# HGRN2 stage: the diagonals of the heads' own scores on ScalarE, behind the squares of the head in front, in place of VectorE

## What is computed

```python
q, fz, i, g = jnp.split(x @ w_in, 4, axis=-1)
q = jax.nn.silu(q)
f = lower_bound + (1.0 - lower_bound) * jax.nn.sigmoid(fz)
log_f = jnp.log(f)
k = 1.0 - f
...
rel = b[:, :, :, None, :] - b[:, :, None, :, :]
decay = jnp.exp(jnp.where(causal[:, :, None], rel, -jnp.inf))
scores = jnp.einsum('bhtk,bhsk,bhtsk->bhts', qc, kc, decay)
intra = jnp.einsum('bhts,bhsv->bhtv', scores, vc)
...
o = rms_norm(o, g_norm).reshape(B, S, D_MODEL) * jax.nn.silu(g)
return o @ w_o
```

## Time and profile before

| | |
|---|---|
| median of 3 runs | 968.34 us (968.09 to 968.36) |
| the profiled execution, its time | 967.88 us |
| its span | 966.1 us |
| granted TensorE clock, mean over the span | 0.999 of full speed |
| TensorE busy | 956.1 us, 99% |
| VectorE busy | 848.8 us, 88% |
| ScalarE busy | 564.8 us, 58% |
| GpSimd busy | 37.9 us, 4% |

### The profile page before, as it was taken

How to read it: one execution, slowest core, us unless ns; L and a number is a source line. 1 busy time by engine, 2 the same in 40 slices (tenths; PEclk the granted TensorE clock), 3 DMA queues, 4 the chain that set the end, 5 groups by cost and what they waited for, 6 DMA issues and landing times.

```text
span 966.1 us, 12770 instructions
## 1 busy us (share of the span) xinstructions
PE 956.1 (99%) x4520; PEld 792.9 (82%) x4520; DVE 848.8 (88%) x1208; ACT 564.8 (58%) x627; POOL 37.9 (4%) x64
## 2 busy tenths in 40 slices
PE   9999999999999999999999999999999999999996
PEld 7888888888888888888888888888888888888885
DVE  5999888996888999899899998999898998888896
ACT  6665556436645555565565555549898545565650
POOL 0100000000210000000000000000100100000000
PEclk9999999999999999999999999999999999999999
DMA  9686566553657565665566565735233655565631
GB/s 305 221 267 239 195 199 222 190 181 125 225 196 237 179 213 179 213 217 174 177 216 216 174 218 179 257 113 192 88 132 121 228 196 193 180 215 176 214 133 43
DMA packets 129312, 184.47 MB, mean 191 GB/s; under 512 B 5968, under 2 KB 104800, under 8 KB 129136
## 3 DMA queue, kind: packets, MB, share of 16 engines
q1 hardware_dynamic: 126032, 173.56, 54.5%
q0 software_dynamic: 2672, 9.77, 2.8%
q10 hardware_dynamic: 560, 0.52, 0.2%
HBM read 182.78 MB, written 1.05 MB: 190 GB/s over the span
## 4 chain that ended last, share of the span: by engine, by line
PE 95%; DVE 3%; ACT 1%; issue 0%; DMA 0%; POOL 0%; DVEq 0%; ACTq 0%
PE psum L1711 29%; PE psum L1720 29%; PE psum L1715 29%; PE psum L1886 2%; PE psum L2235 1%; PE psum L1704 1%; PE psum L2221 1%; DVE w_lo L937 0%; DMA raw<-in_ffn_w_in 0%; ACT w_hi L482 0%; PE psum L1970 0%; PE psum L1990 0%; PE psum L2207 0%; DVE w_lo L967 0%; PE psum L2039 0%
## 5 line engine op out<-in xcount | busy, mean ns | idle before, releaser
L937 DVE TENSOR_TENSOR w_lo<-raw,w_hi 128x2048 fp32r<-128x2048 f32 x125 | 284.8, 2282 | 7.5 <-ACT w_hi L482 7.3
L1711 PE MATMUL psum<-w_hi,xT 128*128 128x512 f32 x959 | 266.1, 394 | 0.6 <-DVE arena L1469 0.4
L1720 PE MATMUL psum<-w_hi,xT 128*128 128x512 f32 x959 | 261.7, 390 | 0.2 <-DVE xT L1011 0.2
L1715 PE MATMUL psum<-w_lo,xT 128*128 128x512 f32 x959 | 261.5, 389 | 0.0
L482 ACT CAST w_hi<-raw 128x2048 fp32r<-128x2048 f32 x125 | 238.7, 1916 | 23.0 <-DMA raw<-in_ffn_w_in 16.1
L1720 PEld LDWEIGHTS psum<-w_hi,xT 128*128 128x128 f32 x959 | 180.1, 188 | 38.5 <-DVE xT L1011 0.5
L1715 PEld LDWEIGHTS psum<-w_lo,xT 128*128 128x128 f32 x959 | 180.0, 188 | 37.6
L1711 PEld LDWEIGHTS psum<-w_hi,xT 128*128 128x128 f32 x959 | 176.8, 188 | 37.4 <-DVE ffn_tok L1069 1.3
L519 ACT ACTIVATE ffn_tok<-psum 128x256 f32<-128x256 f32 x88 | 33.8, 384 | 204.3 <-PE psum L1715 195.4
L1711 PE MATMUL psum<-w_hi,hT_hi 128*128 128x512 f32 x316 | 99.5, 403 | 0.0
L1715 PE MATMUL psum<-w_lo,hT_hi 128*128 128x512 f32 x316 | 95.6, 391 | 0.0
(11 more groups left out here) (202 smaller groups left out, 817.9 us busy)
## 6 DMA issues: line engine op xcount, KB each, us to landing
raw<-in_ffn_w_in SPq DMA_DIRECT2D x170, 512.0 KB, 4.8
raw<-in_ffn_w_out SPq DMA_DIRECT2D x88, 512.0 KB, 4.0
raw<-in_c_w_in SPq DMA_DIRECT2D x32, 512.0 KB, 4.5
raw<-in_ab_w_in SPq DMA_DIRECT2D x16, 512.0 KB, 4.8
raw<-in_ab_w_o SPq DMA_DIRECT2D x8, 512.0 KB, 3.7
raw<-in_c_w_o SPq DMA_DIRECT2D x8, 512.0 KB, 3.7
ln_gb<-in_ln_gain POOLq DMA_DIRECT2D x6, 512.0 KB, 6.4
ln_gb<-in_ln_bias POOLq DMA_DIRECT2D x6, 512.0 KB, 7.2
```

Source lines behind the costliest of these rows:

```text
L937: nc.vector.tensor_tensor(w_lo[:, slot_of[n]], raw[:, n % RAW], w_hi[:, slot_of[n]].bitcast(F32), ALU.subtract).then_inc(lo_ready, 1)
L1711: nc.tensor.matmul(dst, a_hi, b_hi, start=first, stop=False)
L1715: ins = nc.tensor.matmul(dst, a_hi, b_lo, start=False, stop=final and last)
L1720: ins = nc.tensor.matmul(dst, a_lo, b_hi, start=False, stop=final and last)
```

## The change

`head_own` moves from VectorE's queue to ScalarE's. There it is an ACTIVATE Copy of the identity with `kq_own` as its scale. For head 0 it stands behind the copy of the transposes, for every other head behind the squares of the head in front. It waits for the sums (`own_sums`) and for the outputs of the head in front, which read `scT`. VectorE's first masked copy of a head now waits for `own_ready` in place of VectorE's own step.

```diff
@@ semaphores
+            "own_sums", "own_ready",
@@ ScalarE, mix_c
                 head_kqT(0)
+                head_own(0)
                 split(3)
...
                 head_squares(0)
+                head_own(1)
                 log_decay(1)
...
                 head_squares(2)
+                head_own(3)
                 head_kqT(4)
...
                 head_squares(5)
+                head_own(6)
                 head_norm(5)
...
                 head_squares(6)
+                head_own(7)
                 gates(1, 0, G[0])
@@ ScalarE
+            def head_own(hd):
+
+                act.wait_ge(S["own_sums"], 2 * (hd // 2) + 2)
+                if hd:
+                    act.wait_ge(S["head_done"], hd)
+                for t in range(TT):
+                    own = kq_own[:, (hd // 2) % 2, t, hd % 2:hd % 2 + 1]
+                    ins = nc.scalar.activation(scT[:, t], ident[:], ACT.Copy, scale=own)
+                ins.then_inc(S["own_ready"], 1)
@@ VectorE, mix_c
                 logf_split(0)
-                own = head_own(0)
                 split(3)
...
                 lower_factors(6)
-                own = head_own(6)
                 split(12)
-                lower_scores(6, upper_scores(6, own))
+                lower_scores(6, upper_scores(6))
                 head_gate(0, 0, 0, 2)
                 head_gate(0, 1, 0, 2)
-                own = head_own(7)
                 split(13)
@@ VectorE, decays
-                step(ins)
+                ins.then_inc(S["own_sums"], 1)
+                dve.wait_ge(S["own_sums"], 2 * g + t + 1)
@@ VectorE
-            def head_own(hd):
-
-                if hd:
-                    dve.wait_ge(S["head_done"], hd)
-                for t in range(TT):
-                    own = kq_own[:, (hd // 2) % 2, t, hd % 2:hd % 2 + 1]
-                    ins = nc.vector.tensor_scalar(scT[:, t], ident[:], own, None, ALU.mult)
-                steps[0] += 1
-                ins.then_inc(dve_step, 1)
-                return steps[0]
...
-                dve.wait_ge(dve_step, written)
+                if written is not None:
+                    dve.wait_ge(dve_step, written)
...
-            def upper_scores(hd, written):
+            def upper_scores(hd):
 
                 dve.wait_ge(S["levels_done"], 2 * hd + 1)
+                dve.wait_ge(S["own_ready"], hd + 1)
+                written = None
```

More of the change, by code:

```diff
@@ L758, in mix_c @@
                 head_squares(1)
+                head_own(2)
                 sigmoids(2, 1, G[1])
@@ L777, in mix_c @@
                 head_squares(3)
+                head_own(4)
                 head_norm(3)
@@ L786, in mix_c @@
                 head_squares(4)
+                head_own(5)
                 log_decay(3)
@@ L1393, in mix_c @@
                 split(4)
-                lower_scores(0, upper_scores(0, own))
+                lower_scores(0, upper_scores(0))
                 split(5)
                 queries(1, 0, G[0])
-                own = head_own(1)
                 decays(1, 0)
@@ L1402, in mix_c @@
                 decays(1, 1)
-                lower_scores(1, upper_scores(1, own))
+                lower_scores(1, upper_scores(1))
                 logf_split(1)
-                own = head_own(2)
                 split(6)
@@ L1410, in mix_c @@
                 queries(2, 0, G[0])
-                lower_scores(2, upper_scores(2, own))
+                lower_scores(2, upper_scores(2))
                 queries(2, 1, G[1])
@@ L1416, in mix_c @@
                 lower_factors(3)
-                own = head_own(3)
                 split(8)
-                lower_scores(3, upper_scores(3, own))
+                lower_scores(3, upper_scores(3))
                 logf_split(2)
-                own = head_own(4)
                 split(9)
@@ L1425, in mix_c @@
                 split(10)
-                lower_scores(4, upper_scores(4, own))
+                lower_scores(4, upper_scores(4))
                 queries(3, 0, G[0])
                 decays(3, 0)
-                own = head_own(5)
                 upper_factors(5)
@@ L1433, in mix_c @@
                 decays(3, 1)
-                lower_scores(5, upper_scores(5, own))
+                lower_scores(5, upper_scores(5))
                 logf_split(3)
@@ L1450, in mix_c @@
                 split(14)
-                lower_scores(7, upper_scores(7, own))
+                lower_scores(7, upper_scores(7))
                 oT_split(0)
```

## The result

The kernel before took 968.09 us (median of 9 runs, 967.39 to 968.37), the changed one 970.64 us (9 runs, 969.58 to 971.90): 1.0024 of before, interval 1.0015 to 1.0033. That is 2.55 us, so slower by a little over the 0.2% that a measurement of this kernel can tell. The prediction was 970.8. The profiled execution of the changed kernel took 969.58 us with a span of 967.9, against 967.88 and 966.1 before. It is the fastest of its nine runs, so its trace holds 1.7 to 1.8 us of the 2.55.

What follows compares the result with a forecast made beforehand. TensorE bounds the HGRN2 stage, VectorE and ScalarE less than 1 us behind in places. Terms of 0.85 + 1.6 = 2.45 us on the median of 968.34 gave 970.8 us, range 969.4 to 971.4.

Steps and rivals of the forecast that it cites:

- Prices: VectorE sheds 3.2 us; on ScalarE one ACTIVATE takes 0.40 us, a pair 0.70, and 0.60 to the next start.
- Step 1: Head 0: the pair delays ScalarE's CAST, so VectorE's split(3) and the load behind it, then ScalarE, are 0.59 us late.
- Step 2: Head 1: the pair delays the table load, which ends last; the Ln and TensorE's outputs are 0.72 us late.
- Step 3: Head 3: the pair makes ScalarE 1.32 us late; TensorE's transposes wait, and some 0.45 is swallowed at the exponents.
- first term: Heads 0 to 3: TensorE's lateness from ScalarE's added pairs, +0.85 us (0.3 to 1.3).
- Step 4: Head 5: without its pair VectorE's split(12) starts earlier and holds GpSimd's POW to its end, 2.0 us late.
- Step 5: Head 7: exponentials 2.0 us late, VectorE's factors at 746.97 (+1.66), TensorE takes the scores about 1.6 us later.
- second term: Heads 5 to 7: GpSimd held by VectorE's split makes TensorE late at head 7, +1.6 us (0.8 to 1.75).
- GpSimd slips through: Rival, head 5: the POW reads its operands past the split, leaving only the first term, 969.2 us; chance 0.22.
- Hidden in full: Rival: head 0's pair is covered by ScalarE's idle time and GpSimd is free, time stays at 968.3 us; chance 0.09.
- Faster: Rival: VectorE sheds 3.2 us and TensorE's late starts go, at best 967.2 us; chance 0.06.
- Worse: Rival: a shifted split holds GpSimd in one more head, or a late raw load costs 1 to 2 us: 972.3; chance 0.08.

Runs made afterwards that it cites:

- The order-alone kernel: The kernel before with nothing moved to ScalarE; on VectorE head 6's diagonals stand behind split(12) in place of ahead of it: 969.67 us, 1.0020 of before.
- The kernel with head 0 alone: The kernel before with only the diagonals of head 0 moved from VectorE to ScalarE: 968.40 us, 1.0002 of before.
- the three given-back heads: The changed kernel with the diagonals of heads 0, 1 and 6 made on VectorE again: 967.84 us, 1.0000 of before.

## Why the prediction was right

Its time was 0.2 us off, and its mechanism and place of the larger part hold. The closeness of the time is in part luck. The sum has one term that was too large by half a us (the traces hold 2.07 us and not 2.45), and the medians differ by half a us more than the traces account for.

- **Prices.** Forecast 0.40 us for one ACTIVATE, 0.70 for a pair, 0.60 to the next start. Measured 397 ns, 0.68 to 0.70, and 0.60 (654.08 to 654.68). Right. Nothing is idle in front of them, so the new semaphores are free.
- **Step 1** was half right, and this is **the step that failed**. VectorE's split(3) does wait for the CAST and starts at 656.61, from the stage's start 0.54 late (forecast 0.59). The load behind it is issued 0.54 late as well. But "this idle time is no cushion: it moves with the load" took a wait read from one trace for a fixed one. In the changed kernel ScalarE's copy in front of the CAST is 0.60 late, but the CAST at 664.42 follows it with no wait, only 0.11 later than before. None of the five kernels with head 0's pair on ScalarE has this wait. Of the eight with the pair on VectorE, four have it (0.45, 0.32, 0.26 and 0.23 us) and four don't, though all eight have the same order of work up to this place. The order-alone kernel and the kernel before with the squares moved, both the kernel before up to here:

```profile
664.47 1.91 ACT L482 CAST w_hi<-raw 128x2048 fp32r<-128x2048 f32 x1 [0.26 <-DMA raw<-in_c_w_in]
...
664.00 1.92 ACT L482 CAST w_hi<-raw 128x2048 fp32r<-128x2048 f32 x1
```

The length of the issues doesn't explain it: 1.60 us, 1.15 and 1.53 in these three, 0.94 in the changed kernel. So the wait scatters from trace to trace. Whether the landing follows the split by its full 0.54 stays open; the load did not hold ScalarE.
- **Step 2** thus got too much. ScalarE reached the pair of head 1 on time, and the table load, 0.70 later, ended at 676.23. VectorE, 0.60 late since head 0's factors, had shed the 0.40 of its own pair for head 1. Its result for the Ln, before and changed:

```profile
675.98 0.43 DVE L1478 SCALAR_TENSOR_TENSOR arena<-arena,ln_gb 128x256 f32<-128x256 f32 x1
...
675.84 0.42 DVE L1490 SCALAR_TENSOR_TENSOR arena<-arena,ln_gb 128x256 f32<-128x256 f32 x1
```

This is 0.19 late from the stage's start, ends at 676.26, 0.03 behind the table load, and the Ln starts at 676.30. The Ln and TensorE were 0.19 late in place of 0.72, and by VectorE, where the step had put the table load last. The step had left VectorE's relief out. The kernel with head 0 alone shows its size: without the relief VectorE and the Ln are 0.6 late.
- **Step 3.** To the 0.19 comes the pair of head 3, 0.60: TensorE's transposes 0.79 late (forecast 1.32), of which 0.43 are swallowed before the exponents (forecast 0.45). The mechanism was right, **the first term was 0.36 and not 0.85**.
- **Step 4** was right: an operation that ran free beside the pair is held to the end of the split, and the norm is 2.1 us late (forecast 2.0, or 2.1 if both operations are held). It was not the POW that the split held but the TENSOR_SCALAR in front of it, recorded at 736.29, 0.03 us behind the split's start. The split had started 0.01 later than forecast, GpSimd 0.02 later. The Trainium skill's rule (SBUF — State Buffer, section "Who interferes with whom") holds for this half: the operation that came second stood until the split's end, and the POW came behind it. Its other half is against the traces again: with head 6's pair given back, the split began at 737.41, inside the POW of 737.30 to 738.04, and took 2.28 us.
- **Step 5** was right: factors of head 7 at 747.08 (forecast 746.97), and TensorE's outputs late by a second term of 1.71 (forecast 1.6). TensorE has a part of it as a wait for the last factors, 0.52 us at 750.59, and waits once for the cross copy, 0.21 at 753.57, as the step's aside had it.

The rivals fall by single kernels. GpSimd slips through: 2.31 us. Hidden in full: it is what the three given-back heads make (967.84), and not this change. Faster: the pair in head 0 was to cost under 0.1, and alone it costs TensorE 0.6. Worse: in no other head is GpSimd newly held. In head 7 its operation takes 2.17 us where it took 1.85, and TensorE loses no more time behind it.

The median differs by 2.55 us and the two terms add up to 2.07. The profiled execution was the fastest of nine, and the runs of the changed kernel are spread over 2.3 us where the nine of before are over 1.0. This spread is not the change's own: the 27 runs of the kernel before that were timed beside head 0's pair alone go from 967.16 to 970.24. Some of it lies ahead of the stage, which begins anywhere from 631.43 to 633.55 in the thirteen traces, after the same work. Whether the missing 0.5 us come from there stays open.

## What to carry to other kernels

Work taken off an engine is also a delay taken out of its queue: look at what then starts earlier, and whom it shuts out. Here 0.4 us less on VectorE started a long operation with two SBUF inputs on top of a 0.19 us operation of GpSimd, and cost 1.7 us. Where a small operation of GpSimd is on a path, put it, by the order of the queues, where no such VectorE operation can meet it. One such move in head 1 gained 0.9 us, where the five harmless pairs of the change gained nothing that shows.

## What was new about the hardware

A GpSimd operation recorded 0.02 to 0.03 us behind the start of VectorE's two-input split is held to its end like one that comes much later (2.31 us each time, in four kernels). A POW recorded 0.10 or 0.11 us ahead of the split neither held it nor was held to its end: it took 0.74 us, against 0.69 to 0.70 alone, and the split its usual 2.27 to 2.28 (nine kernels). So some 0.1 us in the order of two starts may decide over 2 us. The two are different operations of GpSimd, though, and no trace has a start between these.

The wait for one load was 0.45 us in one trace, 0.23 to 0.32 in three and nothing in four, all with the same order of work in front of it. Idle time in front of a load's consumer, read from one trace, isn't a fixed distance.

Two scalings that nobody needs made a kernel some 2 us faster.
